# Moving parked gate projections into the triangular inversion of a two-layer hybrid block, and the conditioning pairs out of it

## The reference, cut to what matters

```
shift, scale, gate = split(silu(c) @ w_ada + b_ada, 3)       # "conditioning", also for c_ctx
h = rms_norm(x, norm_g) * (1 + scale) + shift
(conv_val, conv_glu, ..., mgate) = split(h @ w_in, IN_SPLITS)
proj = einsum('btnw,nwd->btnd', [y_conv, y_delta, y_attention], w_branch)
x_new = x + gate * (sum_n(sigmoid(mgate_n) * proj_n) @ w_out)
```

## Time and profile before

| what | value |
|---|---|
| median of 3 runs | 1927.29 us |
| the profiled execution, its own time | 1927.93 us |
| its span, first to last instruction | 1926.1 us |
| mean granted TensorE clock | 0.973 |
| PE busy | 1799.3 us (93%), 11060 matmuls |
| PEld, DVE, ACT, POOL busy | 1497.2, 1127.7, 971.5, 669.2 us |
| DMA | 178.86 MB, mean 93 GB/s |

### The profile page before, as it was taken

One profiled execution on the slowest core, in us unless ns is written; L12 is line 12 of the kernel. 1 busy time (PEld: TensorE's weight loads), 2 busy tenths in 40 slices (PEclk: granted clock), 3 DMA queues, 4 the chain that ended last, 5 costly groups with the idle time before them and its releaser, 6 DMA issues. The chain is left out here.

```text
span 1926.1 us, 27717 instructions
## 1 busy us (share of the span) xinstructions
PE 1799.3 (93%) x11060; PEld 1497.2 (78%) x11060; DVE 1127.7 (59%) x1610; ACT 971.5 (50%) x1297; POOL 669.2 (35%) x490
## 2 busy tenths in 40 slices
PE   6789996899999999999999978999798999999999
PEld 5678886898888888888788857878696787777777
DVE  5556495459667656553234255749759866465343
ACT  6657523336445455553653156753337564555661
POOL 0011421537743434453153000144346544433150
PEclk9899998999999999999999999999799999999999
DMA  7123224422221122233244213324222221212352
GB/s 300 34 77 110 72 72 146 133 67 59 95 77 44 55 72 75 82 104 116 89 129 163 96 54 96 98 78 121 78 67 66 77 66 55 72 50 91 106 186 87
DMA packets 76414, 178.86 MB, mean 93 GB/s; under 512 B 6464, under 2 KB 29312, under 8 KB 76160
## 3 DMA queue, kind: packets, MB, share of 16 engines
q1 hardware_dynamic: 34272, 122.46, 20.6%
q10 hardware_dynamic: 42016, 54.63, 8.3%
HBM read 156.00 MB, written 21.07 MB: 92 GB/s over the span
## 5 line engine op out<-in xcount | busy, mean ns | idle before, releaser
L506 PE MATMUL banks<-hH,wHs 128*128 128x512 f32 x1984 | 599.0, 364 | 46.9 <-DVE hL L474 20.5
L506 PE MATMUL banks<-hH,wLs 128*128 128x512 f32 x1984 | 582.8, 355 | 0.0
L506 PE MATMUL banks<-hL,wHs 128*128 128x512 f32 x1984 | 581.1, 355 | 0.0
L1973 POOL TENSOR_TENSOR wLs<-raw,wHs 128x512 fp32r<-128x512 f32 x272 | 410.8, 1536 | 465.2 <-ACT wHs L872 465.2
L506 PEld LDWEIGHTS banks<-hH,wHs 128*128 128x128 f32 x1984 | 327.0, 191 | 123.6 <-issue 26.1
L506 PEld LDWEIGHTS banks<-hL,wHs 128*128 128x128 f32 x1984 | 324.8, 191 | 55.5 <-issue 2.2
L506 PEld LDWEIGHTS banks<-hH,wLs 128*128 128x128 f32 x1984 | 324.6, 191 | 54.7
L872 ACT ACTIVATE wHs<-raw 128x1024 fp32r<-128x1024 f32 x210 | 219.7, 1053 | 219.4 <-DMA raw<-wstream 219.2
L1529 DVE SCALAR_TENSOR_TENSOR acc<-padc,vecs,acc 128x783 f32<-128x783 f32 (+1 forms) x240 | 294.6, 1281 | 0.0
L861 ACT ACT_TABLE_LOAD x180 | 230.9, 1283 | 30.2 <-issue 13.0
L906 ACT ACTIVATE Pa<-banks,stat 128x768 f32<-128x768 f32 (+1 forms) x80 | 64.6, 813 | 144.0 <-DVE stat L1467 144.0
(11 more groups left out here) (242 smaller groups left out, 2330.8 us busy)
## 6 DMA issues: line engine op xcount, KB each, us to landing
raw<-wstream SPq DMA_DIRECT2D x210, 512.0 KB, 3.6
araw<-wstream SPq DMA_DIRECT2D x16, 512.0 KB, 12.6
E<-g_rows ACTq DMA_DIRECT2D x16, 384.0 KB, 7.0
egb<-eg_rows ACTq DMA_DIRECT2D x20, 256.0 KB, 4.2
inb<-intra_rows ACTq DMA_DIRECT2D x20, 256.0 KB, 4.5
parked_logits<-sg ACTq DMA_DIRECT2D x13, 384.0 KB, 4.1
xs<-xT SPq DMA_DIRECT2D x8, 384.0 KB, 11.4
intra_rows<-E ACTq DMA_DIRECT2D x8, 384.0 KB, 3.1
```

Of the source, the lines that this page charges most:

```text
L506: last = pe.matmul(out[:, a:b], w, m[:, kt, a:b], start=(kt == 0 and j == 0), stop=(kt == kts - 1 and j == 2))
L1973: ins = pool.tensor_tensor(wL[w % RING][:, o:o + 512], raw[w % RING][:, o:o + 512], wH[w % RING][:, o:o + 512].bitcast(F32), ALU.subtract)
```

## The change

`LEAF_PARKS` becomes (6, 8). In layer 0 three leafparks stay beside the leaves, and three more stand between the upper levels, where the six pairs stood: one after `five`, one after `fiveb`, one after `six`. The six pairs go into six of the seven slots of attention's head 0, one each; the three pairs of head 3 move to its first, fifth and sixth slot. Three parks leave head 3 (seven become four). In layer 1 eight leafparks stand beside the leaves; one park leaves head 1 and one head 3. `ada_lead` is 1 for all pairs. The parks' buffers are now `gl`: leafpark 0 waits for VectorE's product of `glu` 2, leafpark 1 for that of `glu` 3, instead of for the last store of `E`. The wait of ScalarE at `six` for all the stores goes; VectorE waits for the last two before its first scan step, because `vn` lies where `gl` lay.

```diff
-LEAF_PARKS = (3, 6)
+LEAF_PARKS = (6, 8)
...
-        early, late = late[:6], late[6:]
+        parks = [("leafpark", l, 2, d) for d in range(LEAF_PARKS[l])]
+        beside, between = (parks[:3], parks[3:]) if l == 0 else (parks, [])
...
-        out += leaf[:3] + [glu[2]] + leaf[3:6] + [glu[3]] + leaf[6:7]
-        out += [("leafpark", l, 2, d) for d in range(LEAF_PARKS[l])] + leaf[7:]
-        out += early[:2] + [("five", l)] + early[2:4] + [("fiveb", l)] + early[4:5]
-        out += [("six", l, 1), ("six", l, 0)] + early[5:] + [("sixb", l, 1), ("sixb", l, 0)]
+        out += leaf[:3] + [glu[2]] + leaf[3:6] + [glu[3]] + leaf[6:7] + beside + leaf[7:]
+        out += [("five", l)] + between[:1] + [("fiveb", l)] + between[1:2]
+        out += [("six", l, 1), ("six", l, 0)] + between[2:] + [("sixb", l, 1), ("sixb", l, 0)]
...
-            plan = [["q"], ["k"] + some(g, 1), ["sq"] + some(g, 1), ["v"] + some(g, 1), ["rq", "sk"] + some(g, 1),
-                    ["t"] + some(g, 1), ["rk"] + some(g, 1)]
+            plan = [["q"], ["k"] + some(a, 1) + some(g, 1), ["sq"] + some(g, 1) + some(a, 1), ["v"] + some(a, 1) + some(g, 1),
+                    ["rq", "sk"] + some(a, 1) + some(g, 1), ["t"] + some(a, 1) + some(g, 1), ["rk"] + some(a, 1) + some(g, 1)]
...
-            n = len(park) - 6
-            plan = [some(u, 1) + some(a, 1)] + [some(u, 1) for _ in range(2)] + [some(u, 1) + some(a, 1)]
-            plan += [some(u, 1), some(u, n - 5) + some(a, 1), some(u, 1)]
+            plan = [some(u, 1) + some(a, 1)] + [some(u, 1) for _ in range(3)] + [some(a, 1), some(a, 1), []]
...
-                plan = [["q"], ["k"], ["sq", "v"], ["rq", "sk"] + some(u, 1), ["t"] + some(u, 1) + ["rk"] + some(u, 2 - h)]
+                plan = [["q"], ["k"], ["sq", "v"], ["rq", "sk"] + some(u, 1), ["t"] + some(u, 1) + ["rk"]]
...
         def ada_lead(l, m):
-            return RING if l == 0 or m < 2 else 1
+            return 1
...
-                    if g == 1:
-                        for d in range(LEAF_PARKS[l]):
-                            act.wait_ge(*done("park", l, 2, d))
...
-                    if d < 2:
-                        act.wait_ge(*done("iout", l, 3, 0))
-                        act.wait_ge(*done("iout", l, 3, 1))
-                    else:
-                        act.wait_ge(*done("park", l, n_, d - 2))
-                    act.activation(early[d % 2][:, 0:n], place[u][:, 0:n], ACT.Copy).then_inc(*tick_read("act", u))
+                    act.wait_ge(*(done("glu", l, 2 + d) if d < 2 else done("park", l, n_, d - 2)))
+                    act.activation(gl[d % 2][:, 0:n], place[u][:, 0:n], ACT.Copy).then_inc(*tick_read("act", u))
...
+                    if s == 0:
+                        for d in range(LEAF_PARKS[l] - 2, LEAF_PARKS[l]):
+                            dve.wait_ge(*done("park", l, 2, d))
```

More of the change, by code:

```diff
@@ L350, in build @@
         T1a = arena("T1a", [P, NP, LEAF], B4 + 2 * T3 + 8192)
-        early = [arena("early%d" % i, [P, TOK], (26 + i) * T3) for i in range(2)]
         PT6 = arena("PT6", [P, NP, 64], 24 * T3)
@@ L1246, in _ @@
                     act.wait_ge(*done("pe", u))
-                    if d < 2:
-                        act.wait_ge(*done("iout", l, 3, 0))
-                        act.wait_ge(*done("iout", l, 3, 1))
-                    else:
-                        act.wait_ge(*done("park", l, n_, d - 2))
-                    act.activation(early[d % 2][:, 0:n], place[u][:, 0:n], ACT.Copy).then_inc(*tick_read("act", u))
+                    act.wait_ge(*(done("glu", l, 2 + d) if d < 2 else done("park", l, n_, d - 2)))
+                    act.activation(gl[d % 2][:, 0:n], place[u][:, 0:n], ACT.Copy).then_inc(*tick_read("act", u))
                     act.wait_ge(*done("read", u, 0))
-                    act.dma_start(pscr[l, n_ // 2, d, :, 0:n], early[d % 2][:, 0:n]).then_inc(
+                    act.dma_start(pscr[l, n_ // 2, d, :, 0:n], gl[d % 2][:, 0:n]).then_inc(
                         *tick("leaf_out%d" % (d % 2), "park", l, n_, d, by=16))
```

## The result

The changed kernel takes 1933.52 us (median of 9 runs, 1930.12 to 1938.63), the kernel before, measured beside it, 1925.40 (9 runs, 1923.66 to 1928.23): a ratio of 1.0044, 95% interval 1.0032 to 1.0055. It is slower by 8 us, where 1923 was forecast with 1933 as the upper end.

The account below looks back on a forecast made before the run. TensorE was taken as the limit in layer 0's attention and beside the leaves, with holes at the upper levels. Terms -4.3 - 12.4 + 5 + 11 + 7 - 10.6 gave -4.3, so 1923.0 us; range 1909 to 1933.

Parts of the forecast that it names:

- A: Layer 0 between the upper levels: parks there fill holes and hide part of the pauses, 4.3 us less.
- C: Head 0 of layer 0's attention: new waits for pairs' weights, +4.4 in the fourth slot, 0.6 elsewhere, +5 us.
- D: End of head 3: second adjacent pair 7.7 us late, `az` unit 3 us late, together +11 us.
- E: Layer 1, leaves and upper levels: idle before leafpark 5, upper levels taking 19.5 us, +7 us; bounds +3 and +13.
- F: Attention of layer 1: two parks out, slightly offset by values coming sooner, -10.6 us.
- B: Attention of layer 0: three parks out, -25.5, six pairs in, +13.1, together -12.4 us.
- Rival 4: Head 0: GpSimd becomes the limit, all six slots wait 4.4 us each, 26 instead of 5: 1944; chance 0.12.
- The block: Layer 1: ScalarE's leafpark 1 copy waits for VectorE's `glu` 3 product, holding later weight roundings; TensorE stops at 1348.1.
- the relief: Layer 1: three low parts fall away during ScalarE's wait, so VectorE's leaf instructions shorten, 5.8 us in all.
- Rivals 1: Small groups run freely: no pauses in layer 0, full clock in layer 1's levels: 1915; chance 0.22.
- 2 (no waits): Weights keep up: C is 0, D only its first wait at less than its price, 8 less: 1915; chance 0.13.
- 3 (no relief): Layer 1: VectorE's leaf instructions stay long for another reason, E is 13: 1929; chance 0.08.

Follow-up runs that it names:

- All_beside: Changed kernel with all six leafparks of layer 0 beside the leaves, none between the levels: 1937.10 us, ratio 1.0075 to the kernel before.
- the spread kernels: Layer 0's small matmuls put among the parks' matmuls: by eights in the changed kernel, 1933.52 us; in blocks of 72 in combined, 1908.88 us.
- head0_pair_first: Changed kernel with gate and pair exchanged in the third slot of head 0: 1936.35 us, ratio 1.0065 to the kernel before.
- Tail_lead: Changed kernel with ada_lead giving the whole ring for layer 1's last two pairs: 1930.13 us, ratio 1.0030 to the kernel before.
- combined: Changed kernel with old leafpark buffers in layer 1, head 0's slot exchanged, whole-ring lead, and a park between head 3's last two pairs: 1918.61 us, ratio 0.9969.
- the second profile: The changed kernel measured again without any edit: 1933.58 us, ratio 1.0052 to the kernel before.
- Own_buffers: Changed kernel with its eight layer 1 leafparks in the two buffers the kernel before used: 1928.94 us, ratio 1.0019 to the kernel before.
- before_eight: Kernel before with eight instead of six leafparks in layer 1, in its own buffers, and two parks less in attention: 1917.43 us, ratio 0.9967.
- seven_parks: Own_buffers with seven leafparks in layer 1 and nine parks in attention: 1929.95 us, ratio 1.0031 to the kernel before.

## Why the prediction was wrong

Each wait that was forecast stood where it was said to stand, and nothing idle appeared in heads 1 and 2. The sum failed on sizes, nearly all in one direction: A by 3.2, C by 3.9, with 1.3 ahead of it, D by 2.5, E by 5.6, F by -0.8. The steps that failed are two: that the pauses of the small matmuls would shrink behind a park (A) or stay as they were (E), and that a wait costs only its idle time (A, C, D).

**A.** The step that failed is "a park ahead of a group may hide part of one", by which I took the middle of 0.8 and 8.6. All_beside and the spread kernels show that a park before or behind does not help: it takes part in the pause, as at 310.07. Only matmuls of the park *among* the small ones do. Both pauses stayed at 6.3 of 7.8, the case that I had priced at -0.8, and the second drew a park at the lower clock level after it. The first pause drew one too: the two parks took 10.3 (without the pause) and 10.5 us, with 8.51 forecast. That was paid for by a shorter wait for `egb` (4.05 instead of 5.3) and shorter pauses. Measured -1.1.

**B** was not measured by itself; C and D are counted with it at its forecast price. **F** was right within 0.8.

**C.** The fourth slot's wait was 2.65 us instead of 4.4, in its place and by its cause (head0_pair_first took it away). The "0.6 in the other slots" was mis-sized: 0.6 at slot 6, 2.2 at a bank that ScalarE still read, and 2.7 of lower clock after the first wait. I counted idle time only. That last term is this execution's: with the same wait, four of the eight profiles show none of it; in seven of them the lower level came at the wait of slot 6, in this one it did not. Head 0 took 129.8 to 131.3 us in the eight. Rival 4, GpSimd as the limit of all six slots, did not come: POOL is busy for 73 of 131 us.

**D.** 7.45 and 3.94 against 7.7 and 3: right in the first, 0.9 short in the second. The rest of the missing 2.5 us is the clock (3.75 for the pair instead of 2.04); the `az` unit behind it, 10.13 us instead of 8.7, lies outside D. Tail_lead confirms the order of ScalarE as cause for 7.4 of 13.5, less than "D follows from the order alone"; what the other 6 would need is open, since a park between the pairs (combined) did not win them.

**E.** The block, the relief, and 5.4 us of idle time (5.07) held; leafparks 5 to 7 took 19.35 us where 18.0 was forecast (19.0 in the second profile, 18.1 in tail_lead's). What failed is "I take 19.5, since the pauses remain" for the upper levels: they took 23.8. The pauses did not remain, they grew from 1.5 to 5.7 us. Own_buffers and before_eight have the same without any block, so it belongs to parks that go right up to the level; seven_parks, with 4.3 us of idle time, has 3.1. That idle time before the level is worth something I read in no row: the earlier trace rows show 9.7 us of standing still, and I took them for waste alone. Why it is worth something stays open.

The Trainium skill's rule (TensorE: Matmul & The Clock Gate, "Loop structure matters more than you think") would have put E at its low bound, since back-to-back parks keep the clock up. The granted clock was 0.60 in the first 7.3 us of leafparks 5 to 7, 1.00 in the next 12.0, and then 0.64 in the upper levels; so the parks did bring it back, as the rule says, and it fell again at the levels' first pauses, 1.19 and 2.71 us. The trace does not bear out that eight parks right up to `five` keep the upper levels at the full level.

The relief of VectorE held to the instruction: at 1324.45, before ScalarE's block, a leaf instruction of 300 elements took 1.45 us beside a low part, and the one before it 0.47. During the block they run at the short time (1345.38 above). The Trainium skill (SBUF — State Buffer, "SBUF: two separate sides") says that GpSimd and VectorE share a port pair that one instruction locks for its whole length when VectorE has two inputs in SBUF and GpSimd reads SBUF; the trace agrees with a delay there, of 0.98 us for this instruction.

Rivals 1 (no pauses), 2 (no waits) and 3 (no relief) are out by the rows above. Between them and the forecast there was no case in which all terms lie at their costly side together, though one cause, the lower clock level after an idle time, runs through A, C, D and E.

## What to carry to other kernels

Price a new wait of TensorE by its idle time plus what the work behind it may lose at the lower clock level: here 1 to 3 us after waits of 3.9 us or more, and 0 to 2.7 us after one of 2.65, by the execution. Groups of hundreds of small matmuls can pause with nothing to wait for, here together with the arrival of their instructions; work placed before or after them does not hide that, work put among them does, in blocks of 72 and not of eight, since each turn between small and large costs some tenths of a microsecond. Before a filler is moved into a new place, look whether its buffer ties two engines together: the gain in layer 1 was 5 us with the old buffers and nil with the new ones.

## What the runs showed of the hardware that was not expected

- TensorE's pauses called issue fall together with the packets of the instruction queue (q8, 16 KB each by the page: 1.46 MB in 89). In layer 1 five of them came in 23.8 us (changed) and in 22.5 (before), in both for the same small matmuls. That they limit the group fits every trace read here and was not shown by itself: that more of them can't be had at a time was not tried.
- TensorE's idle time ahead of such a group goes with a shorter group: 9.7 us of idle, 35.2 and 35.3 to the scan; 4.3, 35.6; none, 37.0 to 38.8. By which means, is open.
- Alternating 16 matmuls of 32 x 32 with one of 128 x 512 makes the small ones start 0.43 us behind the large one. Blocks of 72 avoid nearly all of it.
- Waits of about 3 us may or may not be followed by the lower clock level: after the same 2.63 to 2.65 us it came in four profiles of eight, after tail_lead's 3.01 and 2.72 it did not, after 7.45 it came each time.
- Medians and single profiles need not agree: the profiled execution of all_beside took 1930.4 us and its median is 1937.1, and head0_pair_first got shorter in its trace and not in its median. The mean granted clock lay between 0.966 and 0.981 over the runs of the twelve, and one kernel's executions differ by 3 to 12 us.
